# Odd attention: one multiply of every two moves from VectorE to GpSimd

## What is computed

```python
# heads 0..7
logits = jnp.einsum('bhqd,bhkd->bhqk', q_i, k) * ATTN_SCALE
logits = logits + f_i[..., :, None] - fcum[..., None, :]
logits = jnp.where(kpos[None, :] <= qpos[:, None], logits, -jnp.inf)
# heads 8..15
l_own = jnp.einsum('bhqd,bhld->bhql', q_i, k_own) * ATTN_SCALE
l_own = jnp.where(dist_own >= 0, l_own + bias_own, -jnp.inf)
# both
p = jax.nn.softmax(logits, axis=-1)
out = p @ v
y = out @ w_out
```

## Time and profile before

| | |
|---|---|
| time, median of 3 runs | 1242.11 us (1241.94 to 1242.13) |
| profiled execution | 1241.86 us, its span 1240.2 us |
| busy share of the span | PE 99%, PEld 86%, DVE 78%, ACT 57%, POOL 11% |
| granted TensorE clock | 1.00 of full speed |
| the attention loop in the profile | about 347.4 to 378.1 us from the span's start |

### The profile page before, as it was taken

One profiled execution on the slowest core, in us unless ns is written; L12 is line 12 of the kernel. 1 busy time (PEld: TensorE's weight loads), 2 busy tenths in 40 slices (PEclk: granted clock), 3 DMA queues, 4 the chain that ended last, 5 costly groups with the idle time before them and its releaser, 6 DMA issues.

```text
span 1240.2 us, 18559 instructions
## 1 busy us (share of the span) xinstructions
PE 1226.8 (99%) x7013; PEld 1062.9 (86%) x7013; DVE 967.9 (78%) x1218; ACT 703.7 (57%) x1061; POOL 135.2 (11%) x249
## 2 busy tenths in 40 slices
PE   8999999999999999999999999999999999999998
PEld 7989888888778989998889888888888998888887
DVE  5868999977885798898788688997685898676654
ACT  6555555556465555555677566555564243755552
POOL 5000000010000211111132201120010010000000
PEclk9999999999999999999999999999999999999999
DMA  9746777665562798893132348997466597386540
GB/s 325 236 153 218 241 248 238 223 200 180 186 202 68 235 329 311 313 334 115 55 120 71 137 169 293 392 392 261 170 200 208 171 316 259 124 291 212 179 161 34
DMA packets 153649, 265.77 MB, mean 214 GB/s; under 512 B 6092, under 2 KB 110480, under 8 KB 153584
## 3 DMA queue, kind: packets, MB, share of 16 engines
q1 hardware_dynamic: 134560, 204.75, 48.9%
q0 software_dynamic: 18544, 59.65, 13.6%
q10 hardware_dynamic: 480, 0.49, 0.1%
HBM read 263.78 MB, written 1.08 MB: 214 GB/s over the span
## 4 chain that ended last, share of the span: by engine, by line
PE 87%; DVE 8%; ACT 2%; issue 2%; POOL 1%; DMA 0%; POOLq 0%; ACTq 0%; DVEq 0%
PE ps L1949 24%; PE ps L1929 17%; PE ps L1932 9%; PE ps L1915 4%; PE ps L1914 4%; PE ps L1913 4%; DVE w_lo L1142 2%; PE ps L1992 2%; PE ps L1994 2%; PE ps L1993 2%; PE ps L2056 2%; PE ps L1970 2%; PE ps L1972 2%; PE ps L2058 2%; PE ps L1971 2%
## 5 line engine op out<-in xcount | busy, mean ns | idle before, releaser
L1142 DVE TENSOR_TENSOR w_lo<-raw,w_hi 128x2048 fp32r<-128x2048 f32 (+3 forms) x211 | 434.1, 2072 | 32.2 <-ACT w_hi L580 31.9
L580 ACT ACTIVATE w_hi<-raw 128x2048 fp32r<-128x2048 f32 (+3 forms) x213 | 368.7, 1737 | 61.7 <-PE ps L1949 51.1
L1929 PE MATMUL ps<-xn,w_hi 128*128 128x512 f32 x976 | 244.7, 393 | 0.1
L1929 PEld LDWEIGHTS ps<-xn,w_hi 128*128 128x128 f32 x976 | 178.2, 188 | 35.5 <-issue 1.6
L1932 PEld LDWEIGHTS ps<-xn,w_lo 128*128 128x128 f32 x976 | 133.1, 190 | 9.6
L1932 PE MATMUL ps<-xn,w_lo 128*128 128x256 f32 x976 | 136.1, 282 | 0.0
L1949 PE MATMUL ps<-w_hi,a_hi 128*128 128x512 f32 x432 | 134.6, 393 | 0.2 <-DVE a_lo L1854 0.2
L661 ACT ACTIVATE work<-ps 128x512 f32<-128x512 f32 x61 | 36.3, 595 | 171.7 <-PE ps L1932 171.7
L1949 PE MATMUL ps<-w_lo,a_hi 128*128 128x512 f32 x432 | 133.5, 390 | 0.0
L1949 PE MATMUL ps<-w_hi,a_lo 128*128 128x512 f32 x432 | 133.2, 389 | 0.0
L1913 PE MATMUL ps<-xn,w_hi 128*128 128x256 f32 x432 | 122.6, 284 | 0.0
(11 more groups left out here) (362 smaller groups left out, 2006.6 us busy)
## 6 DMA issues: line engine op xcount, KB each, us to landing
raw<-in_ffn_w SPq DMA_DIRECT2D x64, 1024.0 KB, 5.5
side<-in_ada_w POOLq DMA_DIRECT2D x96, 512.0 KB, 6.1
raw<-in_ffn_w_in SPq DMA_DIRECT2D x40, 1024.0 KB, 5.2
raw<-in_ffn_w_out SPq DMA_DIRECT2D x32, 512.0 KB, 5.2
raw<-in_gm_w_in SPq DMA_DIRECT2D x16, 1024.0 KB, 6.4
raw<-in_od_w_in SPq DMA_DIRECT2D x12, 1024.0 KB, 5.5
raw<-in_gm_w_out SPq DMA_DIRECT2D x8, 1024.0 KB, 5.5
raw<-in_ev_w_in SPq DMA_DIRECT2D x7, 1024.0 KB, 13.3
```

Of the source, the lines that this page charges most:

```text
L580: nc.scalar.activation(w_hi[s][:, 0:w], raw[s][:, 0:w], ACT.Copy).then_inc(hi_done, 1)
L1142: nc.vector.tensor_tensor(w_lo[s][:, 0:w], raw[s][:, 0:w], w_hi[s][:, 0:w].bitcast(F32), ALU.subtract)\
L1929: nc.tensor.matmul(o, hi, xn[:, 512 * k:512 * k + 512], start=k == 0, stop=False)
```

## The change

For each pair of heads the even one is normalized on VectorE as before. For the odd one VectorE makes the reciprocals only and raises the new semaphore `at_over`; it does not wait for its own reciprocal there. GpSimd waits for `at_over` and multiplies the two segments in place with two instructions, each of which raises `made`. TensorE's `at_weights` of an odd head waits for `made` instead of `at_p`. 32 multiplies on VectorE become 16, and 16 stand on GpSimd.

GpSimd's stream changes around them. The multiplies of heads 1 and 3 come behind the four `side` loads and ahead of the bias loads; that of head 5 comes between the third bias load and the fourth, that of head 7 behind the fourth, those of heads 9 to 15 one after the other. Two semaphores are merged with others to make room (`neg` into `f`, `half_ready` into `made`), which moves nothing.

```diff
             def at_probs(i):
 
-                dve.wait_ge(AT["exp"], 2 * i + 2)
-                c, one_over = 34 + 4 * (i % 4), 48 + 2 * (i % 4)
-                chain(nc.vector.reciprocal(st[:, one_over:one_over + 2], st[:, c:c + 2]))
-                for t, (c0, c1) in enumerate(SEG):
-                    s = at_sb[i % 4][:, c0:c1]
-                    nc.vector.tensor_scalar(s, s, st[:, one_over + t:one_over + t + 1], None, ALU.mult).then_inc(AT["p"], 1)
+                for n in (i, i + 1):
+                    dve.wait_ge(AT["exp"], 2 * n + 2)
+                    c, one_over = 34 + 4 * (n % 4), 48 + 2 * (n % 4)
+                    over = nc.vector.reciprocal(st[:, one_over:one_over + 2], st[:, c:c + 2])
+                    if n % 2:
+                        over.then_inc(AT["over"], 1)
+                        break
+                    chain(over)
+                    for t, (c0, c1) in enumerate(SEG):
+                        s = at_sb[n % 4][:, c0:c1]
+                        nc.vector.tensor_scalar(s, s, st[:, one_over + t:one_over + t + 1], None, ALU.mult).then_inc(AT["p"], 1)
...
             for i in range(0, HEADS, 2):
                 if 2 <= i < HEADS - 2:
                     at_probs(i + 2)
-                    at_probs(i + 3)
...
             def at_weights(i):
-                pe.wait_ge(AT["p"], 2 * i + 2)
+                if i % 2:
+                    pe.wait_ge(made, i + 2)
+                else:
+                    pe.wait_ge(AT["p"], i + 2)
...
             for c in range(SLOTS):
                 side_load(U_FFN1 + c, ada_view(0, 2 + c, 0))
+
+            def at_probs(n):
+
+                pool.wait_ge(AT["over"], n // 2 + 1)
+                for t, (c0, c1) in enumerate(SEG):
+                    s, k = at_sb[n % 4][:, c0:c1], 48 + 2 * (n % 4) + t
+                    nc.gpsimd.tensor_scalar(s, s, st[:, k:k + 1], None, ALU.mult).then_inc(made, 1)
+
+            at_probs(1)
+            at_probs(3)
             pool.wait_ge(w_used, T_V + 4)
             for part in range(2):
                 bias_load([y[:, 0:2, :] for y in t5_late], part, 2).then_inc(rb_ready, 16)
             for part in range(2):
                 bias_load([y[:, 2:6, :] for y in t5_late], part, 4).then_inc(rows_out, 16)
+                at_probs(5 + 2 * part)
+            for n in range(9, HEADS, 2):
+                at_probs(n)
             pool.wait_ge(AT["a_ready"], HEADS // 2)
```

More of the change, by code:

```diff
@@ L359, in build @@
         vec_ps, vec_ready, cs_ready = sem("vec_ps"), sem("vec_ready"), sem("cs_ready")
-        rb_ready, half_ready, rows_ps, rows_sb, rows_out = sem("rb_ready"), sem("half_ready"), sem("rows_ps"), sem("rows_sb"), sem("rows_out")
+        rb_ready, made, rows_ps, rows_sb, rows_out = sem("rb_ready"), sem("made"), sem("rows_ps"), sem("rows_sb"), sem("rows_out")
         bias_in, ctx_in = sem("bias_in"), sem("ctx_in")
@@ L379, in build @@
         RELU = [group(f"relu{n}", "sq", "ahi", "a_ready") for n in range(2)]
-        AT = group("at", "qk", "v_sb", "v_act", "z_ps", "zt", "z", "nabs", "ez", "ln", "neg", "f_ps", "f", "sel", "s_ps", "s_sb",
+        AT = group("at", "qk", "v_sb", "v_act", "z_ps", "zt", "z", "nabs", "ez", "ln", "over", "f_ps", "f", "sel", "s_ps", "s_sb",
                    "max", "exp", "p", "t_ps", "pt", "o_ps", "ohi", "a_ready")
@@ L1491, in _ @@
             dve.wait_ge(AT["ln"], 1)
-            nc.vector.tensor_tensor(zf[:, 3, :], zf[:, 1, :], zf[:, 2, :], ALU.subtract).then_inc(AT["neg"], 1)
+            nc.vector.tensor_tensor(zf[:, 3, :], zf[:, 1, :], zf[:, 2, :], ALU.subtract).then_inc(AT["f"], 1)
             chain(nc.vector.memset(gate_row.bitcast(F32), 0.0))
@@ L1506, in _ @@
                 split(T_QK + j + 4)
-            dve.wait_ge(AT["f"], 1)
+            dve.wait_ge(AT["f"], 2)
             dve.wait_ge(rows_out, 16)
@@ L1517, in _ @@
             gain_cols(24, sums[:, 8:16], 0, 1, g_mix).then_inc(mod_ready, 1)
-            for i in range(4):
+            for i in (0, 2):
                 at_probs(i)
@@ L2220, in _ @@
                 if j == 5:
-                    pe.wait_ge(AT["neg"], 1)
+                    pe.wait_ge(AT["f"], 1)
                     nc.tensor.matmul(ps[6][:, 0:8], tri_ones[:, 0:P], zf[:, 3, 0:8], start=True, stop=True)
@@ L2292, in _ @@
             pe.wait_ge(join_done, J_QK + 5)
-            pe.wait_ge(AT["f"], 1)
+            pe.wait_ge(AT["f"], 2)
             pe.wait_ge(AT["sel"], 1)
@@ L2666, in _ @@
                 pool.dma_start(stage[p:p + m, r, :], src).then_inc(in_later, 16)
-            nc.gpsimd.memset(half[:, :], -0.5).then_inc(half_ready, 1)
-            pool.wait_ge(half_ready, 1)
+            nc.gpsimd.memset(half[:, :], -0.5).then_inc(made, 1)
+            pool.wait_ge(made, 1)
             row_rstd("ev")
```

## The result

The changed kernel takes **1246.16 us** (median of 7 runs, 1245.90 to 1246.84) against 1241.96 for the kernel before in the same comparison (7 runs, 1241.73 to 1242.68): a ratio of 1.0035, 95% interval 1.0026 to 1.0044. It is slower by 4.2 us. The profiled execution took 1246.16 us, its span is 1244.5.

What follows compares the result with a forecast made beforehand. The prediction took a circle of waits through TensorE, ScalarE and VectorE to bound the attention loop. Heads 7, 9, 11 and 13 at +1.0 us each and head 15 at +0.2 made 1242.1 + 4.2 = 1246.3 us, range 1242.8 to 1247.8.

Steps and rivals of the forecast that it cites:

- The circle of waits: Attention loop: odd head's transposes, ScalarE's copy and next exponentials, VectorE's reciprocals, multiplies, next transposes; 3.53 us, forecast 4.5.
- The way from reciprocals to transposes: Odd head: reciprocals 0.17, GpSimd's wake-up 0.17, two multiplies 1.41, TensorE's wake-up 0.05; 1.80 us instead of 0.80.
- The row that the price rested on: Profile row of GpSimd's same multiply on 512 columns, 1.57 us; gave 0.54 us for 128 columns, 0.88 for 256.
- the memset: GpSimd's memset of 256 columns in 0.35 us, the lower bound for an odd head's two multiplies: 0.76 us.
- Head 5's 1.0 us: Head 5's transposes come 1.0 us later, but VectorE's relief cancels it before head 7's exponentials; nothing in the sum.
- Heads 1 and 3: Their GpSimd multiplies ahead of the loop, beside VectorE's splits, cost TensorE 0 to 0.2 us; head 3 ready at 349.2.
- no such exclusion: In the loop VectorE doesn't keep GpSimd's multiplies out, since it reads scores from PSUM beside them; no cost.
- The bias loads: Issued later on GpSimd, first three at worst 1.4 us; they cost nothing, the fourth with little to spare.
- (a): Rival: GpSimd multiplies at the memset's pace, 0.76 us for an odd head; +0.9 us, 1243.0 us; chance 0.16.
- (b): Rival: VectorE's relief wins outright, with GpSimd's two multiplies under about 0.5 us; 1241.6 us; chance 0.05.
- (c): Rival: fourth bias load lands late, at 367.2, delaying scores of heads 12 and 13; +1.1, 1247.4 us; chance 0.07.
- (d): Rival: TensorE's own work bounds the loop, its waits aren't real; 4 x 0.8 = 3.2, 1245.3 us; within the forecast's 0.72.

Runs made afterwards that it cites:

- a4: The changed kernel with GpSimd's 256 columns done in two instructions of 128, three multiplies per head; 1247.96 us, ratio 1.0045.
- b2: The kernel before with head 9 alone multiplied on GpSimd, all other heads on VectorE; 1243.05 us, ratio 1.0006.
- a1: The changed kernel with ScalarE, from turn 4 on, taking the next even head's exponentials before copying out the odd head; 1243.96 us, ratio 1.0016.
- a2: The kernel before with ScalarE, from turn 4 on, taking the next even head's exponentials before copying out the odd head; 1241.95 us, ratio 0.9998.
- b4: The changed kernel with two more reciprocals, read by nobody, on VectorE behind each odd head's reciprocals; 1246.38 us, ratio 1.0034.
- b5: The changed kernel with heads 1 and 3 left on VectorE, so GpSimd multiplies odd heads 5 to 15 only; 1246.37 us, ratio 1.0033.
- d1: The changed kernel with GpSimd multiplying only an odd head's 128 columns and VectorE the 256 at the same time; 1242.82 us, ratio 1.0005.
- a3: The changed kernel with the even heads multiplied on GpSimd and the odd ones on VectorE; 1245.19 us, ratio 1.0024.

## Why the prediction was right

**The time.** 1246.3 was forecast, 1246.16 came. In the rows of the profiled executions: a sum of 4.2 us, 4.25 measured at head 15.

**The circle of waits** is what the runs confirm: a4 lengthens it by what GpSimd's multiply is longer, b2 shows that one head costs 1.0 us for good, and a1 gives over half of the loss back by shortening it elsewhere. a2, the same order in the kernel before, takes away a part of its small waits. TensorE's own 3.38 us are what the prediction took them for, 3.53 less 0.15. The spacing went from 3.53 to the forecast 4.5.

**The way from reciprocals to transposes**: 1.80 forecast, 1.81 measured. Two of its terms were off and cancelled: the multiplies took 1.50 us and not 1.41 (0.59 and 0.91, not 0.54 and 0.88), GpSimd woke up in 0.09 and not 0.17. The 0.17 came from a row in which GpSimd waited for its own instruction (`<-POOL rstd`), not for another engine. The row that the price rested on, 512 columns of the same operation, was a good one; the memset was not, since it reads nothing.

**Head 5's 1.0 us** was rightly put at nothing, for the wrong reason. The prediction had "the gain from the relieved VectorE is there: it cancels the whole 1.0 us of head 5". The exponentials of head 6 did come at 356.43 (forecast 356.42) and those of head 7 at 357.31 (357.3), but b4 shows them at the same distances with two thirds of the relief taken back. The step should have read: ScalarE has 0.97 us of slack there, so the late head 5 falls into it. The relief itself was also larger than the 0.46 us forecast: the scoring of head 6 starts at 353.71 instead of 354.31. It was worth nothing, because the late head 5 had already used up the waits that it would have ended.

**Heads 1 and 3**: 0 to 0.2 forecast, and none that b5 can tell. VectorE let GpSimd in earlier than I had assumed: head 3 was ready at 347.84, not 349.2. The Trainium skill (SBUF — State Buffer, Who interferes with whom) says that a VectorE instruction with two inputs in SBUF holds the read port that GpSimd needs, and one with a single input and outside the two-port modes doesn't. The trace agrees on the first: 3.91 us for 128 columns beside the splits. A single input alone is no safe sign: beside one VectorE multiply with one input in SBUF, 256 columns in 0.35 us, GpSimd lost 0.17 us in d1; no run shows in which mode that multiply is.

For the loop the prediction said that no such exclusion arises, since VectorE reads scores from PSUM there. The outcome was right, the reason not quite: beside head 5's multiply (353.90 to 355.40) VectorE also takes head 6's row maxima from a buffer in SBUF,

```profile
354.60 0.61 DVE L1468 TENSOR_REDUCE st<-acc 128x1 f32<-128x128 f32 x2
```

and GpSimd needed the same 1.50 us as for the other heads.

**The bias loads**: all four landed in 4.5 to 9.0 us, and nobody waited for them:

```profile
who waited for it (us, times):
...
DMA to landing us min/median/max: 4.5/7.8/9.0
```

**The rivals.** (a), the memset's pace, falls: 1.50 us are twice its 0.76. With it falls, for this operation, what the Trainium skill (GPSIMD Engine Reference, § 4.1 Engine selection) says of one-input work at roughly line rate: VectorE does both segments in 0.55 us, GpSimd in 1.50. The 0.76 was itself too high for its row: 0.351 us for 256 columns, with a fixed 0.19, make 0.6 ns a column and 0.62 us for the two multiplies. (b), a win by VectorE's relief, falls by the same 1.50, where it needed under about 0.5. b4 shows only that the relief is worth nothing behind a head 5 that is 1.0 us late; what it would be worth with a quick GpSimd wasn't run. (c), the late fourth load, falls with the rows above. (d), that TensorE's waits are not real, would have left 0.8 us of each 1.0; the spacing grew by the full 1.00, from 3.53 to 4.53 us, and the 4.2 us are 1.0 more than its 3.2. **Not foreseen** was the clock: the wait that the change makes lowers it in some executions.

## What to carry to other kernels

Before work is moved to an idle engine, the way that goes through it has to be followed: where it closes a circle with the engine that bounds the kernel, its longer time is paid in each turn, and the relief of the other engine is worth only the waits that it ends (here none, since the late piece had used them up). The piece to move is the one that doesn't close the circle, and even that, as a3 shows, has to be followed through the order of the engine that it leaves. If a wait remains anyway, look for an order of the third engine in the circle: on ScalarE two lines moved gave back 2.4 of 4.2 us.

## What the runs showed of the hardware

- GpSimd's multiply by a scalar from SBUF, float32, in place, 128 partitions: 0.594 us for 128 columns, 0.915 for 256. VectorE: 0.55 for both in a row.
- A hand-over from VectorE to GpSimd takes 0.09 us, one from GpSimd to TensorE 0.05.
- GpSimd and VectorE can hold each other up when both work from SBUF to SBUF, by less than the other's whole instruction if that is short. GpSimd took 0.76 instead of 0.594 us beside a VectorE multiply of 0.35, and 3.91 beside two long splits in a row; VectorE's two multiplies took 0.65 to 0.91 instead of 0.55 in a3. Beside VectorE's row maxima from SBUF, and beside its reads from PSUM, GpSimd lost nothing (1.50 us for a head).
- TensorE's granted clock fell from 1.00 to 0.50 for 3.4 us behind a single wait of 1.6 us in a kernel that keeps it busy for 99% of the span. It fell in some executions and not in others of the same kernel, and where nothing hid it the run was 1.2 to 2.7 us longer. With the wait filled with transposes the profile shows 1.00, and none of 11 runs was longer than 1242.73 us. The profile of the changed kernel has such a wait of 1.59 us and shows 1.00.
